# Expert weights in runs of 16 KB per partition, with strided operands on TensorE to match

## The reference

```
logits = xt @ w_router + b_router
top_logits, top_idx = top_k(logits, 4);  top_w = softmax(top_logits)
# for each expert e, over the tokens routed to it:
gu   = xb @ w_gate_up[e] + b_gate_up[e]          # [tokens, 1024] @ [1024, 2048]
gate = min(gate, 7);  up = clip(up, -7, 7)
h    = (up + 1) * gate * sigmoid(1.702 * gate)
y    = (h @ w_down[e] + b_down[e]) * weight      # [tokens, 1024] @ [1024, 1024]
out  = sum of y over the experts of each token
```

## Time and profile before

| | |
|---|---|
| runs, median | 1482.43 us |
| runs, lowest and highest | 1475.98, 1483.13 us |
| profiled execution, span from first to last instruction | 1482.8 us |
| mean granted TensorE clock | 0.964 of full speed |
| TensorE matmul busy | 1388.4 us, 94% of the span |
| TensorE weight loads busy (they overlap matmuls) | 736.0 us, 50% |
| VectorE, ScalarE, GpSimd busy | 28%, 15%, 10% |
| HBM read | 452.55 MB, 306 GB/s over the span |
| stage of the experts | from about 400 us to the end |

### The profile page before, as it was taken

One profiled execution on the slowest core, in us unless ns is written; L12 is line 12 of the kernel. 1 busy time (PEld: TensorE's weight loads), 2 busy tenths in 40 slices (PEclk: granted clock), 3 DMA queues, 4 the chain that ended last, 5 costly groups with the idle time before them and its releaser, 6 DMA issues.

```text
span 1482.8 us, 18166 instructions
## 1 busy us (share of the span) xinstructions
PE 1388.4 (94%) x7611; PEld 736.0 (50%) x7611; DVE 415.3 (28%) x793; ACT 224.4 (15%) x366; POOL 153.6 (10%) x104
## 2 busy tenths in 40 slices
PE   5989999999899999999999999999999999999996
PEld 5879998998543333333333333333333333333332
DVE  5495552446521112021111112211111112111113
ACT  4543253444100000000000000000000000000000
POOL 6133322454200000000000000000000000000000
PEclk9998999999799999899999999999999999999999
DMA  9333322665689999899999999998998999989940
GB/s 315 117 114 114 114 84 89 238 240 202 267 342 375 392 377 376 313 385 387 365 375 375 391 395 396 378 374 356 395 394 358 393 374 395 396 345 385 377 171 29
DMA packets 96795, 454.34 MB, mean 306 GB/s; under 512 B 6237, under 2 KB 10410, under 8 KB 63946
## 3 DMA queue, kind: packets, MB, share of 16 engines
q1 hardware_dynamic: 96746, 453.62, 77.9%
HBM read 452.55 MB, written 1.05 MB: 306 GB/s over the span
## 4 chain that ended last, share of the span: by engine, by line
PE 83%; DVE 12%; issue 2%; ACT 1%; SPq 1%; DMA 1%; POOL 0%; DVEq 0%
PE bank L1273 31%; PE bank L1302 17%; PE bank L1249 9%; PE bank L1257 4%; PE bank L1102 4%; PE bank L1103 4%; PE bank L1104 4%; PE bank L1293 2%; DVE early L1499 2%; DVE late L1642 1%; DVE late L1638 1%; DVE late L1646 1%; PE bank L1287 1%; DVE late L1639 1%; PE bank L1309 1%
## 5 line engine op out<-in xcount | busy, mean ns | idle before, releaser
L1273 PE MATMUL bank<-late 128*64 128x512 f32 x1424 | 328.5, 602 | 2.5 <-issue 2.5
L1273 PEld LDWEIGHTS bank<-late 128*64 128x64 f32 x1424 | 94.8, 136 | 180.4 <-issue 177.5
L1302 PE MATMUL bank<-late 128*64 128x512 f32 x704 | 171.6, 642 | 0.0
L1249 PEld LDWEIGHTS bank<-late,hx 128*128 128x128 f32 x1056 | 127.0, 194 | 53.3 <-issue 53.3
L1273 PE MATMUL bank<-raw,late 128*64 128x512 f32 x624 | 143.5, 603 | 0.8 <-DVE late L1634 0.8
L717 POOL TENSOR_TENSOR w_lo<-raw,w_hi 128x1024 fp32r<-128x1024 f32 x47 | 114.4, 2436 | 220.3 <-ACT w_hi L983 220.3
L1638 DVE TENSOR_SCALAR late<-bank 128x512 f32<-128x512 f32 x32 | 22.1, 692 | 410.3 <-PE bank L1273 410.3
L1249 PE MATMUL bank<-late,hx 128*128 128x64 f32 x1056 | 136.8, 279 | 0.0
L1102 PE MATMUL bank<-act_hi,w_hi 128*128 128x256 f32 x448 | 130.4, 291 | 5.0 <-DVE w_lo L717 4.0
L1103 PE MATMUL bank<-act_lo,w_hi 128*128 128x256 f32 x448 | 127.2, 284 | 0.0
L1104 PE MATMUL bank<-act_hi,w_lo 128*128 128x256 f32 x448 | 127.2, 284 | 0.0
(11 more groups left out here) (311 smaller groups left out, 1230.3 us busy)
## 6 DMA issues: line engine op xcount, KB each, us to landing
late<-in_w_gate_up_dram SPq DMA_DIRECT2D x89, 2048.0 KB, 10.0
late<-in_w_down_dram SPq DMA_DIRECT2D x44, 2048.0 KB, 10.1
raw<-in_w_gate_up_dram SPq DMA_DIRECT2D x39, 2048.0 KB, 9.2
raw<-in_w_down_dram SPq DMA_DIRECT2D x20, 2048.0 KB, 9.5
raw<-in_w_in_dram SPq DMA_DIRECT2D x14, 2048.0 KB, 8.1
raw<-in_w_br_dram SPq DMA_DIRECT2D x3, 2048.0 KB, 8.9
raw<-in_w_o_dram SPq DMA_DIRECT2D x2, 2048.0 KB, 8.6
raw<-in_w_mem_kv_dram SPq DMA_DIRECT2D x4, 512.0 KB, 7.4
```

What stands on the lines that cost most here:

```text
L1249: ins = mm(ps[0][:, k * CAP:(k + 1) * CAP], hx[:, t, k * P:(k + 1) * P], onehot[:, t, :], start=(t == 0), stop=(t == NT - 1))
L1273: ins = mm(bk[64 * c:64 * c + 64, :], x_slotT[:, k, :], w[:, kk, at + 512 * c:at + 512 * (c + 1)], start=False, stop=(k == KD - 1))
L1302: ins = mm(ps[3][64 * c:64 * c + 64, :], hidT[:, kk, 64 * q:64 * q + 64], w[:, kk, c * 512:(c + 1) * 512], start=False, stop=(q == 1 and k ...
```

## The change

The set of rows in a chunk stays the same, 256 rows of gate/up or 512 rows of down. Which partition holds which row changes. Before, partition p held rows p and p+128 of a gate/up chunk (runs of 8 KB in HBM) and rows p, p+128, p+256, p+384 of a down chunk (runs of 4 KB). Now it holds rows 2p and 2p+1, or 4p to 4p+3, which is one run of 16 KB. A matmul over block k then contracts over every second (or every fourth) row, so the other operand must have the same columns: the gather reads `hx` with a step of two elements (8 bytes) and the transposes of the hidden activations read `h_tok` with a step of four elements (16 bytes). Both are stationary operands. Counts and shapes of all instructions of TensorE, the number and size of transfers, the slots and all waits are the same.

```diff
         def chunk_dma(sp, c, gu, dn, dst, landed):
             if c < 4:
-                src = gu.rearrange("(k p) n -> p k n", p=P)[:, 2 * c:2 * c + 2, :]
-                dst = dst.rearrange("p (k n) -> p k n", k=2)
+                src = gu[2 * P * c:2 * P * (c + 1), :].rearrange("(p k) n -> p (k n)", k=2)
             else:
-                src = dn.rearrange("(k p) n -> p k n", p=P)[:, 4 * (c - 4):4 * (c - 4) + 4, :]
-                dst = dst.rearrange("p (k n) -> p k n", k=4)
+                src = dn[4 * P * (c - 4):4 * P * (c - 3), :].rearrange("(p k) n -> p (k n)", k=4)
             sp.dma_start(dst, src).then_inc(landed, 16)
...
             def gather(first=0, last=KD):
                 for k in range(first, last):
                     for t in range(NT):
-                        ins = mm(ps[0][:, k * CAP:(k + 1) * CAP], hx[:, t, k * P:(k + 1) * P], onehot[:, t, :],
+                        own = hx[:, t, 2 * P * (k // 2) + k % 2:2 * P * (k // 2 + 1):2]
+                        ins = mm(ps[0][:, k * CAP:(k + 1) * CAP], own, onehot[:, t, :],
                                  start=(t == 0), stop=(t == NT - 1))
...
                 for c in range(4):
-                    ins = tr(ps[3][:, c * P:(c + 1) * P], h_tok[:, c * P:(c + 1) * P], ident[:])
+                    ins = tr(ps[3][:, c * P:(c + 1) * P], h_tok[:, c:4 * P:4], ident[:])
```

## The result

The changed kernel takes 1518.2 us (median of four runs, 1511.1 to 1525.7), the kernel before in the same comparison 1480.7 us (1476.0 to 1483.1). The ratio is 1.0255, interval 1.0211 to 1.0299: slower by 2.6%. I forecast 1484, most likely no change, range up to 1512. The time lies outside the range. The direction had a chance of 0.37, and the rival that came nearest was one I had written down, at 1504.

What follows compares the result with a forecast made beforehand. TensorE was taken as the bound, with the DMA share high only because TensorE consumes weights at that rate. 1482.4 + 0 (transfers) + 0 (gather) + 2 (transposes) + 0 (clock) = 1484 us, range 1473 to 1512.

Steps and rivals of the forecast that it cites:

- the rival that came nearest: At the transposes of the hidden activations: strided loads slow and the clock drops follow; 1504 us, from 1489 to 1534, chance 0.29.
- Bound and transfers: Experts' stage: TensorE bounds it and never waits for weights; packets fall from 96,795 to 55,835, gain 0.
- the lead of the transfers: Experts' weight chunks land 36 us or more before use, so a transfer loss of less than 9% stays hidden.
- Two of the signs that I had named: Forecast wrong if an undisturbed item exceeds 32.4 us, L1273 or L1302 waits for DMA, or drops change by over four.
- Gather: 32 weight loads per item at a step of 8 bytes: taken as 0, upper end 114 us in all.
- a comparison of columns per time: Gather loads at 8 bytes per 0.87 ns cover no wider memory than transposes now, 4 bytes per 0.42 ns; cost 0.
- the point at which the clock follows: An item longer by about 0.2 us, from which up to all 32 items can have a clock drop, 30 us more.
- Transposes: Four per item at a step of 16 bytes: taken as 0.06 us per item, 2 us in all.
- the forecast's own arithmetic: Transposes' loads: doubled column time overlapping the rest moves the pace from 93 to 108 ns; without overlap 7 us.
- Clock: Lower clock after TensorE's wait and the small transposes: drops stay near 14 of 32 items, change taken as 0.
- kept four either way: Allowance on the number of clock drops: 4 drops more or fewer, 4 x 1.69 = 7 us.

## Why the prediction was wrong

*Bound and transfers: right.* TensorE is the bound, the lead of the transfers covers them, the packets fell as worked out, and the transfers alone changed nothing (0.9972). Two of the signs that I had named for a wrong forecast came true: an undisturbed item above 32.4 us (32.45), and drops that change by more than four (by 16).

*Gather: a term set to 0 that is not.* I took 0 from a comparison of columns per time and measured 7 ns per load, 0.2 us per item, 6 us in all; twice the price of the transposes, which I had taken for the dangerous ones. It is small per load and is multiplied by 32, fully exposed. So the comparison did not carry from one kind of load to the other, and this is what put the item past the point at which the clock follows.

*Transposes: mechanism right, size near.* Taken 0.06 us per item, measured 0.09. The load went up by 72 ns, but the four loads follow each other at (0.56 - 0.21) / 3 = 0.12 us instead of 0.093, so most of the 72 ns is overlapped, as the forecast's own arithmetic allowed. The rule on lines of 16 bytes (the Trainium skill, Advanced Engine Details and Errata, SBUF Cachelines) fits the ordinary loads well: 8 bytes with two hits nearly free (+4 ns), 16 bytes with one hit +137. It does not fit the transposes, which pay in full at 8 bytes already.

*Clock: the step that failed.* I took 0 for it, arguing that without a stretch the drops stay near 14, and kept four either way. The stretch was there, 0.28 us per item instead of my 0.06, and with it the drops went to 30. The rival had the mechanism, a point from which it decides (0.2 us; 0.20 alone was not yet enough) and the observation that after a drop the next item starts nearly in the same place; but I priced it at half of its upper end (15 us) because I did not see that it hardly has a middle: once a dropped item has just the length that repeats, all following items drop. By the two traces the drops add 22.4 us, so 1482.4 + 8.7 + 22.4 = 1513.5; the measured 1518.2 lies higher, with a spread of 1511.1 to 1525.7. I also tied the rival to the transposes alone, and it needed only the length. The prices of both edges have to be added before the rival is judged: 0.09 us alone gives 1.0044, 0.20 alone 1.0087, both 1.0255. With the prices that I had taken (0 and 0.06) the sum stays under the rival's 0.2 us; it was the gather's 0 that kept it there. That the direction of the rival was on the page was judgment; that its 1504 lies within 1% of the measured time is partly luck, as its direct price (7 us for the transposes alone) came from the wrong loads.

Open: the spread of the changed kernel's runs (1511 to 1526). Two of its executions were traced, with spans of 1509.2 and 1515.1 us, and both have 30 drops and no stall like the one around 607 us; 4.9 of the 5.9 us between them arise ahead of the first down stage (426.83 and 431.72), where the second has the lower granted clock (0.91 against 0.95 from 300 to 400 us, 0.74 against 0.87 from there to 426). So part of the spread is the clock in the mixer, which the prediction did not look at. Open too is why a series with drops starts in both of these traces, and in those with operands alone and with two VectorE instructions on the kernel before, but not in each block of the kernels with three more transposes; the traces show only that the stalls at the loop's turn break the series there.

## What to carry to other kernels

In a kernel bound by TensorE, with items of equal length and one thin stretch in each, compare the down stage item by item in the chain: a run of equal long forms means that the clock drops periodically, and then a few tenths of a microsecond per item can decide over 1 to 2%, in either direction. What helped here was to fill the thin stretch with work moved from elsewhere, worth 2.7%, about half of it by the idle time itself. Padding the item gave back 10 us once and cost 8 us the next time; trimming it was not tried. And before a layout is changed for the transfers' sake, ask whether a transfer is ever waited for: here the gain was zero from the start, so any price was too high. Last, a price per instruction is to be multiplied by its count before it is called nothing.

## What was not expected of the hardware

- A weight load of an ordinary float32 matmul at a step of 16 bytes takes 329 ns instead of 192, at 8 bytes 196. That of a transpose takes 140 contiguous and 209 to 212 at either step.
- The drops settle into a rhythm of their own: 34.13 us from drop to drop in the changed kernel (from 34.16 in one trace, from 34.09 in the other), with operands alone (from 34.10), and with two VectorE instructions on the kernel before (34.12 to 34.14).
- 186 more instructions on TensorE over the run (six per item) brought a stall at each turn of the loop of five items, 4.4 to 6.8 us of extra length each, with 75 instead of 30 or 39 instruction packets.
- Runs of 16 KB instead of 4 and 8 KB took 0.94 instead of 0.97 of the DMA engines' time at 390 GB/s, and 0.96 instead of 1.00 at 400.
